# Plain pairs' silu and product moved behind the next pair's work, with buffers of their own

## The reference

```python
def rmsnorm(x, g):
    xf = x.astype(jnp.float32)
    y = xf * lax.rsqrt(jnp.mean(xf * xf, axis=-1, keepdims=True) + RMS_EPS)
    return (y * g.astype(jnp.float32)).astype(x.dtype)

def swiglu(h, w_gate, w_up, w_down):
    return (jax.nn.silu(h @ w_gate) * (h @ w_up)) @ w_down
```

## Time and profile before

| | us |
|---|---|
| median of 3 runs | 2279.35 |
| lowest, highest run | 2278.64, 2291.93 |
| the profiled execution | 2286.9 |
| its span, first to last instruction | 2285.1 |
| TensorE busy | 2155.2 |
| VectorE, GpSimd, ScalarE busy | 1350.8, 1179.1, 946.6 |
| mean granted TensorE clock | 0.977 |

### The profile page before, as it was taken

One profiled execution on the slowest core, in us unless ns is written; L12 is line 12 of the kernel. 1 busy time (PEld: TensorE's weight loads), 2 busy tenths in 40 slices (PEclk: granted clock), 3 DMA queues, 4 the chain that ended last, 5 costly groups with the idle time before them and its releaser, 6 DMA issues.

```text
span 2285.1 us, 40902 instructions
## 1 busy us (share of the span) xinstructions
PE 2155.2 (94%) x14990; PEld 1967.2 (86%) x15007; DVE 1350.8 (59%) x2282; ACT 946.6 (41%) x1891; POOL 1179.1 (52%) x817
## 2 busy tenths in 40 slices
PE   7899999999998888999999899999999998999997
PEld 6898999958766578899999799999997697999997
DVE  5727455778886448636365763637556567455453
ACT  5525344331454325525345542525315435344343
POOL 4738576323201026748575775848641067666671
PEclk9999999999998999999999999999999899999999
DMA  5344453544202441443434252444461032525351
GB/s 128 71 116 103 108 120 94 107 94 99 62 1 77 146 102 38 91 104 79 98 85 99 49 118 65 97 91 91 95 154 29 1 75 56 120 59 117 67 110 42
DMA packets 378148, 197.68 MB, mean 87 GB/s; under 512 B 66532, under 2 KB 374477, under 8 KB 377933
## 3 DMA queue, kind: packets, MB, share of 16 engines
q1 hardware_dynamic: 366108, 180.79, 35.6%
q10 hardware_dynamic: 11552, 13.71, 2.0%
q0 software_dynamic: 288, 0.56, 0.2%
HBM read 192.23 MB, written 11.64 MB: 89 GB/s over the span
## 4 chain that ended last, share of the span: by engine, by line
PE 47%; DVE 9%; issue 3%; ACT 2%; POOL 2%; DMA 0%; DVEq 0%; ACTq 0%; POOLq 0%; SPq 0%
PE psum L1054 7%; PE psum L1056 7%; PE psum L1055 7%; PE psum L1013 6%; PE psum L1014 4%; PE psum L1016 4%; PE psum L1012 4%; PE psum L1015 3%; DVE psum L2343 1%; DVE XT L2374 1%; PE psum L1384 1%; PE psum L1414 1%; PE psum L1400 1%; POOL S L814 1%; PE psum L1380 1%
## 5 line engine op out<-in xcount | busy, mean ns | idle before, releaser
L801 POOL CAST WSP<-WST 128x1024 fp32r<-128x1024 f32 (+1 forms) x41 | 45.1, 1099 | 487.6 <-PE psum L1016 340.1
L834 POOL TENSOR_TENSOR WSP<-WST,WSP 128x512 fp32r<-128x512 f32 x106 | 152.7, 1445 | 140.6 <-ACT WSP L1737 140.6
L1054 PE MATMUL psum<-XT,WSP 128*128 128x288 f32 x656 | 197.8, 302 | 15.9 <-ACT shots L1932 11.2
L1055 PE MATMUL psum<-XT,WSP 128*128 128x288 f32 x656 | 194.6, 297 | 0.0
L1056 PE MATMUL psum<-XT,WSP 128*128 128x288 f32 x656 | 194.2, 296 | 0.0
L1054 PE MATMUL psum<-XS,WSP 128*128 128x288 f32 x552 | 164.5, 298 | 13.8 <-DVE GS L2418 6.1
L2592 DVE SCALAR_TENSOR_TENSOR X<-psum,X 128x576 f32<-128x576 f32 x64 | 48.4, 756 | 204.8 <-PE psum L1016 204.8
L2343 DVE SCALAR_TENSOR_TENSOR psum<-S,WST 128x512 f32<-128x512 f32 x70 | 110.4, 1577 | 96.9 <-POOL S L814 90.4
L1056 PE MATMUL psum<-XS,WSP 128*128 128x288 f32 x552 | 162.8, 295 | 0.0
L1055 PE MATMUL psum<-XS,WSP 128*128 128x288 f32 x552 | 162.7, 295 | 0.0
L1013 PE MATMUL psum<-GS,WSP 128*128 128x512 f32 x406 | 161.1, 397 | 0.0
(11 more groups left out here) (450 smaller groups left out, 7474.1 us busy)
## 6 DMA issues: line engine op xcount, KB each, us to landing
WST<-in_ffn_w_gate SPq DMA_DIRECT2D x148, 256.0 KB, 4.8
WST<-in_ffn_w_down SPq DMA_DIRECT2D x144, 224.0 KB, 4.0
WST<-in_ffn_w_up SPq DMA_DIRECT2D x104, 256.0 KB, 4.1
WSTX<-in_ffn_w_up SPq DMA_DIRECT2D x64, 256.0 KB, 4.3
WSTX<-in_ffn_w_down SPq DMA_DIRECT2D x48, 224.0 KB, 4.1
WST<-in_a_w_in SPq DMA_DIRECT2D x28, 256.0 KB, 4.6
kv0A<-in_cache_kv SPq DMA_DIRECT2D x48, 128.0 KB, 2.3
kv2A<-in_cache_kv SPq DMA_DIRECT2D x48, 128.0 KB, 2.3
```

The costliest lines, as they stand in the source:

```text
L834: nc.gpsimd.tensor_tensor(by_pair(low), raw, by_pair(high).bitcast(F32), ALU.subtract).then_inc(pool_set, 1)
L1054: mm(out, high[:, c], operand(prod, 0, k), start=first and k == 0, stop=False, skip_group_check=True)
L1055: mm(out, high[:, c], operand(prod, 1, k), start=False, stop=False, skip_group_check=True)
```

## The change

1. Every plain pair gets buffers of its own (`plain_rooms[half, p]`), and `up_copy` no longer waits for the pair before.
2. ScalarE: the silu of the plain pairs moves from the start of pair PLAIN (2 in ffn0, else 1) to the place just ahead of that pair's own silu, and `hidden_high` of the plain pairs to just ahead of that pair's `hidden_high`, in the list of the next pair. The high part of P5 is made two steps earlier in ffn0.
3. VectorE: `plain_up`, `plain_hidden` and `plain_low` move behind the preparation of pair PLAIN + 2.
4. P1 of the pair two behind a plain one waits for the gate's evacuation (`gate_set`) instead of the low part (`hidden_set`).
5. GpSimd makes P5's low part and the sum S3 ahead of the last token parts.
6. The statistics matmuls stand behind d = 5 instead of d = 3.
7. The bias copies are issued in twos, ahead of the high part of block d = 4.

The diff, without the lines in which only a room's argument changes:

```diff
         for half in ("up", "gate"):
-            sb(c2, "before_" + half, [P, DB - 2, TOK])
-            plain_rooms[half + "_back"] = sb(c2, "back_" + half, [P, TOK])
-            plain_rooms[half] = sb(c2, "plain_" + half, [P, TOK])
+            sb(c2, "before_" + half, [P, DB - 4, TOK])
+            for p in (1, 0):
+                plain_rooms[half + "_back", p] = sb(c2, f"back_{half}{p}", [P, TOK])
+                plain_rooms[half, p] = sb(c2, f"plain_{half}{p}", [P, TOK])
...
@@ GpSimd, start @@
                     if k == 2:
                         low_of_raw(name, p, "P2")
-                    elif k == 3:
                         low_of_sum(name, p, "P5")
+                        sum_first(name, p)
                     token_low(i, k, 1)
-                sum_first(name, p)
                 low_of_sum(name, p, "P7")
@@ TensorE, plain_pair and p1 @@
-                        if d == 3:
+                        if d == 5:
                             statistics(e)
...
-                if n > 1:
+                if p > 1 and plain(name, p - 2):
+                    pe.wait_ge(gate_set, 2 * (n - 1))
+                elif n > 1:
                     pe.wait_ge(hidden_set, 2 * (n - 1))
@@ ScalarE, up_copy and update @@
                 act.wait_ge(w_used, DONE[name, p, "up"])
-                if n:
-                    act.wait_ge(hidden_set, 2 * n)
...
                     if k == 1:
                         root(e)
-                high_of(to, PLAIN[to], "P5")
+                    elif k == 2:
+                        high_of(to, PLAIN[to], "P5")
@@ ScalarE, ffn @@
                         p = PLAIN[name]
-                        for k in range(p - 1):
-                            silu(name, k)
-                            hidden_high(name, k)
                         if name == "ffn0":
                             up_copy(name, p - 1)
                             high_of(name, p, "P6")
                             high_of(name, p, "P3")
+                        high_of(name, p, "P7")
                         shot_1(name, p)
-                        high_of(name, p, "P7")
-                        silu(name, p - 1)
+                        high_of(name, p, "P4")
                         shot_5(name, p)
-                        hidden_high(name, p - 1)
-                        high_of(name, p, "P4")
                         next_high(p, "P1")
...
                     next_high(p, "P2")
+                    if q == 0:
+                        for k in range(p):
+                            silu(name, k)
                     silu(name, p)
...
                         shot_2(name, p)
+                        if q == 0 and p == first + 1:
+                            for k in range(first):
+                                hidden_high(name, k)
                         hidden_high(name, p - 1)
...
                     hidden_high(name, p)
+                    if tail and q < THIRDS - 1:
+                        tail(2 * q)
+                        tail(2 * q + 1)
                     high_of_down(name, q, AHEAD + 1)
                     if q < THIRDS - 1:
                         for d in range(AHEAD + 2, ND):
                             high_of_down(name, q, d)
-                            if tail and d < AHEAD + 4:
-                                tail(2 * q + d - AHEAD - 2)
@@ VectorE, load_x and ffn @@
                 plain_gate("ffn0", 0)
-                plain_up("ffn0", 0)
                 token_low(0, 3)
-                plain_hidden("ffn0", 0)
-                plain_low("ffn0", 0)
...
                         gate_first(name, p)
-                        plain_up(name, p - 1)
-                        plain_hidden(name, p - 1)
                         sums(name, p + 1)
-                        plain_low(name, p - 1)
...
                             lows_of_sums(name, p + 1)
+                        if q == 0 and p == first + 1:
+                            for k in range(first):
+                                plain_up(name, k)
+                                plain_hidden(name, k)
+                                plain_low(name, k)
                         hidden(name, p - 1)
```

More of the change, by code:

```diff
@@ L530, in shot_count, with plain_room @@
             return 3 * product_pairs(name, p) + (("P5", "P1", "P6") if begins_third(p) else ("P1", "P5", "P6")).index(prod) + 1
-        def plain_room(half):
-            return plain_rooms[half][:, :]
+        def plain_room(half, p):
+            return plain_rooms[half, p][:, :]
         def plain_acc(name, p, half):
@@ L1763, in up_copy @@
             def up_copy(name, p):
-                n, k = pair_number(name, p), plain_acc(name, p, "up")
+                k = plain_acc(name, p, "up")
                 act.wait_ge(w_used, DONE[name, p, "up"])
-                if n:
-                    act.wait_ge(hidden_set, 2 * n)
-                fn(plain_room("up"), acc(k), ACT.Copy)
-                fn(plain_room("up_back")[:, FRONT:TOK], back_parts(k)[:, 1, :], ACT.Copy).then_inc(up_sum, 1)
+                fn(plain_room("up", p), acc(k), ACT.Copy)
+                fn(plain_room("up_back", p)[:, FRONT:TOK], back_parts(k)[:, 1, :], ACT.Copy).then_inc(up_sum, 1)
             def update(e, layer=None, to=None, behind=lambda d: None):
@@ L1939, in silu @@
             def silu(name, p):
-                g = plain_room("gate") if plain(name, p) else gs[:, side(name, p), :]
+                g = plain_room("gate", p) if plain(name, p) else gs[:, side(name, p), :]
                 act.wait_ge(gate_set, 2 * (pair_number(name, p) + 1))
@@ L1945, in hidden_high @@
                 act.wait_ge(hidden_set, 2 * pair_number(name, p) + 1)
-                fn(GH[:, p % DB, :], plain_room("up") if plain(name, p) else bank_ab(name, p), ACT.Copy).then_inc(gh_set, 1)
+                fn(GH[:, p % DB, :], plain_room("up", p) if plain(name, p) else bank_ab(name, p), ACT.Copy).then_inc(gh_set, 1)
             def ffn(name, e=None, to=None, tail=None):
@@ L1990, in ffn @@
                     next_high(p, "P4")
-                    for p in range(p + 1, (q + 1) * DB):
+                    first = p
+                    for p in range(first + 1, (q + 1) * DB):
                         next_high(p, "P1")
@@ L2420, in plain_gate @@
             def plain_gate(name, p):
-                k, dst = plain_acc(name, p, "gate"), plain_room("gate")
+                k, dst = plain_acc(name, p, "gate"), plain_room("gate", p)
                 low, r = back_parts(k)[:, 1, :], rstd[:, :]
@@ L2430, in plain_up @@
             def plain_up(name, p):
-                u = plain_room("up")
+                u = plain_room("up", p)
                 dve.wait_ge(up_sum, pair_number(name, p) + 1)
-                steps.done(tt(u[:, FRONT:TOK], u[:, FRONT:TOK], plain_room("up_back")[:, FRONT:TOK], ALU.add))
+                steps.done(tt(u[:, FRONT:TOK], u[:, FRONT:TOK], plain_room("up_back", p)[:, FRONT:TOK], ALU.add))
                 steps.done(tt(u, u, rstd[:, :], ALU.mult))
             def plain_hidden(name, p):
-                n, u = pair_number(name, p), plain_room("up")
+                n, u = pair_number(name, p), plain_room("up", p)
                 dve.wait_ge(silu_done, n + 1)
-                tt(u, u, plain_room("gate"), ALU.mult).then_inc(hidden_set, 1)
+                tt(u, u, plain_room("gate", p), ALU.mult).then_inc(hidden_set, 1)
             def plain_low(name, p):
-                n, u = pair_number(name, p), plain_room("up")
+                n, u = pair_number(name, p), plain_room("up", p)
                 dve.wait_ge(hidden_set, 2 * n + 1)
```

## The result

| | before | after |
|---|---|---|
| median of 10 runs, us | 2289.11 (2278.64 to 2298.44) | 2274.27 (2273.14 to 2277.23) |
| ratio, 95% interval | 1 | 0.9942 (0.9924 to 0.9961) |
| profiled execution: time, span | 2286.9, 2285.1 | 2277.23, 2275.4 |

The change made the kernel **faster by 0.58%, 13 us of 2289** (9 to 17 by the interval; the two medians lie 15 apart). The predicted 2284 was a loss of 4.5 us, so the direction was wrong. That 2274 lies in the range of 2268 to 2297 is luck: the range was built on a median of three runs, 2279.35, and that of ten is 10 higher. As a difference the range went from 11 us gained to 18 lost, and 13 were gained. Beside the median, the spread fell from 20 us to 4.

A forecast was written before the change was run, and what follows sets the result against it. TensorE, 94% busy, bounds the kernel, so only block starts count. ffn0 +3.9, three other blocks +3.6 and copies -3 make +4.5 us on 2279.35, forecasting 2284; range for 8 in 10: 2268 to 2297.

The forecast's parts named there:

- S2's length: VectorE's S2 at the four block starts: 5.5 us at two, 1.75 at the others, in the new order too.
- my own signs of being wrong: Gaps before P1 of pair first + 2 under 2 us, S2 short throughout there, or ffn0's turns changing over 5 us.
- my own walk: Queues followed with profiled durations at ffn1's start: P7's low part ends at 915.8, S1 of pair 3 at 917.1.
- The copies: Four bias copies on ScalarE's queue in ffn0's first two down stages: moving them gains 3 us in all.
- The starts' chain: Before P1 of pair first + 2: plain steps cost 3.4 us in ffn1 to ffn3, 6.8 in ffn0, against earlier sums.
- The front half: At block starts ScalarE's new order brings S1 of pair 3 in ffn1 3.7 us earlier; ffn0's S1 5.8 earlier.
- The clock: TensorE at half clock behind the longer gap before P1: 1.5 us lost in each of ffn1 to ffn3, 2.9 in ffn0.
- The statistics: Moving two matmuls to d = 5 fills a 2.02 us TensorE gap but is worth nothing at the end.
- The rival "Faster": S2 short at the starts (7.4 us gained), copies give 7, clock costs 1 less: 2271; chance 0.27.

The follow-up runs named there:

- e1: The kernel before with only the four bias copies moved as in the change; 2275.3 us, ratio 0.9955 to before.
- unfenced: Traces of kernels without the added wait that lets GpSimd start P4's low part only after VectorE's S2 of the next pair.
- e8: The changed kernel with the bias copies back in their old place; 2283.5 us, ratio 0.9985 to before.
- e7: The kernel before with the bias copies moved and GpSimd waiting for VectorE's S2 ahead of P4's low part; 2255.4 us, ratio 0.9872.
- e2: The kernel before with one added wait per pair, GpSimd for VectorE's S2 ahead of P4's low part; 2258.4 us, ratio 0.9887.
- the fence pair: The changed kernel with GpSimd's added wait for VectorE's S2 (2263.8 us) against e7 (2255.4), which lacks the rest of the change; 8.4 us slower.
- e13: The changed kernel with ScalarE's old order at the starts (shot_1, P7, silu, shot_5, P4); 2278.0 us, ratio 0.9948 to before.
- e14: The changed kernel with GpSimd's old order at the starts (P5's low part and S3 behind the last token parts); 2283.7 us, ratio 0.9976.
- e9: The changed kernel with the two statistics matmuls back at d = 3; 2273.4 us, ratio 0.9955 to before.
- e16: The changed kernel with P7's high part of pair first + 1 ahead of the silus at the starts; 2271.6 us, ratio 0.9928 to before.
- e17: The kernel before with ScalarE's P7 high part waiting for GpSimd's P2 low part at starts and turns, making GpSimd idle 0.87 us; 2281.8 us, 0.9963.
- e15: The changed kernel with both ScalarE's and GpSimd's old orders at the starts; 2289.3 us, ratio 0.9996 to before.

## Why the prediction was wrong, point by point

- **S2's length: the step that failed.** "I take two in four for the new order too, so it drops out of the sum." In the order of before S2 was long at 6 of 9 starts in ffn1 to ffn3 (7 of 12 with e1); under ScalarE's new order at none of 24 in eight unfenced traces. At 3.7 us each (ffn1's start in e1, where S2 was short, lies 3.75 earlier than in before), 7 in 12 of three starts is 6.5 us gained. One of my own signs of being wrong came true with it (S2 short throughout the starts), and the first turn's 5.7 us was another. I had argued from GpSimd's longer stretch without a wait and overlooked the 0.74 us ahead of P7's low part that the two silus make, though my own walk had it (S1 later than it could be, "behind the table load and now two silus").
- **The copies: mis-sized, and for the same reason.** I took 3, the runs say 10 (e1, e8). Without long forms it is 3 (e7 against e2), the value I took; I had left the long forms out on the ground that "the copies do not make" them. Late weights do bring them about: they put S1 behind the down stage, where VectorE waits for it and GpSimd has four operations ready. Against the measured -13.3 my +4.5 is 17.8 off, and 13.3 of that are these two steps (6.8 and 6.5).
- **The starts' chain: right, somewhat too dear.** P1 of pair 2 in ffn0 at 60.92 (61 to 62); gap before P1 of pair 3 in ffn1 5.83 (5.4), in ffn0 9.33 (8.8); S2 in ffn1 4.4 us earlier (3.7); ffn2, with S2 short in both traces, +1.3 (+1.2). All of it together is 8.4 by the fence pair, where I had 7.5, and 4.8 by the traces below; the median of few runs on either side leaves both possible. ffn0, with 3.9 forecast, lost about 2.0 where no long S2 stood near. The gap before P6 of pair 2, which I had stay at 2.03, shrank to 0.96.
- **The front half: right size, wrong reason.** I gave ScalarE's order the credit; e13 and e14 show that GpSimd's gives it.
- **The clock: right in ffn1, too dear in ffn0.** From P1's first matmul to P6's took 6.79 us in ffn1 (937.59 - 932.11 = 5.48 before), 1.3 lost of 1.5 predicted; 1.9 in ffn2, 0.9 in ffn3. In ffn0 it took 6.71 against 98.26 - 92.79 = 5.47, and 1.2 were lost, not 2.9: the granted clock was 0.50 (1.2 GHz) from 87.80 to 98.00, but for more than half of that TensorE was still waiting. The windows after:

```profile
87.80:98.00 10.20, 4.09 (x17) 0.50 0.04 10
923.10:929.00 5.90, 5.85 (x29) 0.63 0.01 1
```

- **The statistics: right** in the changed kernel, worth nothing that the runs can tell (e9).
- **The rival "Faster"** came closest, 2271 with S2 short at the starts and the copies at 7. I gave it 0.27 against 0.43 because one term could not be read from the trace of before; four instances in one trace were enough to see that the long form has causes, not enough to say that they would persist.

The sum by the measured terms: copies and S2 at the turns -9.8 (e8), the starts' order +4.8 (the changed kernel's second trace against e1, in ffn2 against before, S2 short in each: 2.0 + 1.1 + 1.4 + 0.3), S2 at the starts -6.5: -11.5, against -13.3 (-17.4 to -8.9) measured.

## What to carry to other kernels

An operation whose duration varies by three times between like neighbours is a term, not noise: list every instance with what the contending engine did before and behind it, before assuming that its share stays. Where VectorE waits for GpSimd and GpSimd has more work ready, one wait of GpSimd for VectorE's step costs 0.8 us of GpSimd and gives back 1.1 to 4.8 us of a chain that bounds the kernel (here 25 us in all). Work that is moved out of an engine's way belongs in the idle time of the chain it leaves, not merely behind its former neighbours: the same steps cost 23 us more between S2 and `hidden_low` than in VectorE's idle time ahead of S2.

## What the hardware showed that was not expected

- VectorE's operation with two inputs of SBUF can be shut out by GpSimd for four operations in a row (5.5 us instead of 0.70 alone and 1.75 behind one). The Trainium skill (SBUF — State Buffer, "Who interferes with whom") has the two exclude each other by a lock; by that S2 waits for one operation of GpSimd. The short form agrees (1.75 us), the long form of 5.5 us does not, and the measurement decides.
- The long form followed a run of five or more of GpSimd's operations without a break where four more stood ready (19 of 28), hardly ever a shorter run (4 of 647). Where GpSimd hesitated 0.1 us behind S1 (e16), VectorE got in at once. e17 shows that adding the break removes the long form; which queue or arbiter does this, no run tells. The four exceptions (108.74 in the change, 2062.06 in e1, 2187.33 in e13, 322.42 in e15) are open.
- The four kernels whose traces have long forms at the starts of ffn1 to ffn3 (before, e1, e13, e15) spread over 17 to 20 us, the other thirteen over 3 to 11. A wide spread can be the sign of a wait that occurs in some runs only. It isn't the whole of it: the stretch through mixer B varies as well, and e7 and e14 spread over about 10 us without a long form in their traces.
